# The token factor of the second RMS norm applied to the up projection's sums in PSUM, and another order of the first pairs

## The reference

```python
x = x + jnp.einsum('bse,ed->bsd', y_mix, w_out[l])          # output projection, "OUT"
h = rms_norm(x, norm2_g[l])                                  # x * rsqrt(mean(x*x) + eps) * g
u = causal_dwconv(jnp.einsum('bsd,df->bsf', h, w_up[l]), ffn_conv_w[l])
gate, up = jnp.split(u, 2, axis=-1)
x = x + jnp.einsum('bsf,fd->bsd', jax.nn.gelu(gate) * up, w_down[l])   # down projection, "DOWN"
return rms_norm(x, final_g)
```

## Time and profile before

| | us |
|---|---|
| median of three executions | 1773.47 |
| lowest, highest | 1772.86, 1775.33 |
| the profiled execution | 1773.04 |
| its span, first to last instruction | 1771.3 |
| mean granted TensorE clock in it | 0.982 |
| PE busy | 1705.1 (96%) |
| VectorE busy | 1179.0 (67%) |
| ScalarE busy | 791.0 (45%) |
| GpSimd busy | 538.3 (30%) |

### The profile page before, as it was taken

One profiled execution on the slowest core, in us unless ns is written; L12 is line 12 of the kernel. 1 busy time (PEld: TensorE's weight loads), 2 busy tenths in 40 slices (PEclk: granted clock), 3 DMA queues, 4 the chain that ended last, 5 costly groups with the idle time before them and its releaser, 6 DMA issues.

```text
span 1771.3 us, 20806 instructions
## 1 busy us (share of the span) xinstructions
PE 1705.1 (96%) x7516; PEld 1383.2 (78%) x7516; DVE 1179.0 (67%) x1406; ACT 791.0 (45%) x1022; POOL 538.3 (30%) x297
## 2 busy tenths in 40 slices
PE   6999999999859999999999999998999999999998
PEld 5888878888647888888888888887878877666786
DVE  6577671379888776676676789885636455666554
ACT  5566631245434444444444444553422155666531
POOL 4222122100055455455553000003433242444320
PEclk9999999999879999999999999998999999999999
DMA  7111112063302322322323965651322220110251
GB/s 252 48 47 36 47 48 72 24 220 114 119 11 85 95 73 81 95 71 83 91 75 107 342 217 186 224 160 42 119 72 71 84 71 24 36 48 25 89 220 71
DMA packets 159896, 176.96 MB, mean 100 GB/s; under 512 B 13390, under 2 KB 114516, under 8 KB 159828
## 3 DMA queue, kind: packets, MB, share of 16 engines
q1 hardware_dynamic: 157524, 167.67, 29.4%
q10 hardware_dynamic: 2304, 8.39, 1.3%
HBM read 140.38 MB, written 35.65 MB: 99 GB/s over the span
## 4 chain that ended last, share of the span: by engine, by line
PE 87%; DVE 7%; ACT 3%; issue 1%; POOL 1%; DMA 0%; DVEq 0%; ACTq 0%
PE ps L895 27%; PE ps L2282 25%; PE ps L2230 19%; PE ps L2481 5%; PE ps L2451 3%; PE ps L2466 2%; PE ps L2511 2%; PE ps L2454 2%; PE ps L2453 1%; DVE lat L1993 1%; DVE hop_lo_P L1802 1%; PE ps L2438 1%; DVE hop_mix_P L1796 1%; DVE square_dve L1580 0%; DVE scr L1737 0%
## 5 line engine op out<-in xcount | busy, mean ns | idle before, releaser
L919 POOL TENSOR_TENSOR w_lo<-w_raw,w_hi 128x1024 fp32r<-128x1024 f32 x52 | 136.0, 2617 | 622.5 <-ACT w_hi L1035 622.5
L2282 PE MATMUL ps<-hop_hi_P,wop_hi_P 128*128 128x512 f32 x672 | 266.9, 397 | 25.8 <-DVE hop_lo_P L1802 12.8
L2282 PE MATMUL ps<-hop_lo_P,wop_hi_P 128*128 128x512 f32 x672 | 265.8, 395 | 0.0
L2282 PE MATMUL ps<-hop_hi_P,wop_lo_P 128*128 128x512 f32 x672 | 265.3, 395 | 0.0
L895 PE MATMUL ps<-h_hi,w_hi 128*128 128x512 f32 x752 | 235.6, 395 | 13.3 <-DVE h_lo L1565 9.8
L895 PE MATMUL ps<-h_lo,w_hi 128*128 128x512 f32 x752 | 233.7, 392 | 0.0
L895 PE MATMUL ps<-h_hi,w_lo 128*128 128x512 f32 x752 | 233.4, 392 | 0.0
L925 POOL TENSOR_TENSOR wop_lo_P<-pair_raw,wop_hi_P 128x512 fp32r<-128x512 f32 x72 | 113.3, 1574 | 243.6 <-ACT wop_hi_P L1046 243.5
L895 PEld LDWEIGHTS ps<-h_hi,w_hi 128*128 128x128 f32 x752 | 142.0, 190 | 44.9 <-issue 15.9
L2282 PEld LDWEIGHTS ps<-hop_hi_P,wop_hi_P 128*128 128x128 f32 x672 | 128.7, 192 | 55.1 <-issue 13.6
L925 POOL TENSOR_TENSOR wop_lo_P<-pair_sum,wop_hi_P 128x512 fp32r<-128x512 f32 x96 | 132.0, 1376 | 125.4 <-ACT wop_hi_P L1046 125.4
(11 more groups left out here) (337 smaller groups left out, 3274.4 us busy)
## 6 DMA issues: line engine op xcount, KB each, us to landing
pair_raw<-in_w_up SPq DMA_DIRECT2D x48, 512.0 KB, 4.7
w_raw<-in_w_in SPq DMA_DIRECT2D x46, 512.0 KB, 3.9
dn_raw<-gu_park SPq DMA_DIRECT2D x84, 256.0 KB, 3.9
dn_raw<-in_w_down SPq DMA_DIRECT2D x60, 256.0 KB, 3.1
gu_park<-up_cv SPq DMA_DIRECT2D x24, 512.0 KB, 2.6
out_raw<-in_w_out SPq DMA_DIRECT2D x30, 256.0 KB, 3.0
x_tok<-in_x SPq DMA_DIRECT2D x4, 1024.0 KB, 8.0
x_park<-xs SPq DMA_DIRECT2D x1, 4096.0 KB, 14.7
```

The source lines that it names most:

```text
L919: nc.gpsimd.tensor_tensor(lo[:, :], raw[:, :], hi[:, :].bitcast(f32), ALU.subtract).then_inc(w_lo_done, 1)
L2282: mm = nc.tensor.matmul(dst, w[q][:, k, :], x[q][:, k, :], start=a, stop=b, skip_group_check=True)
```

## The change

- **The norm is taken apart.** ScalarE multiplies x1 by the gain alone (`gained`), partly between the last steps of OUT, into `xs` and, for B22, into `hop_mix["P3"]`. The token factor is spread once for all 1024 tokens, copied by ScalarE from `ps[3]` into SBUF (`rstd_row`, in the T2 half of `xs` tiles 4 and 5), and VectorE multiplies the sums in PSUM with it, 128x1024 in place, once for the gate and once for the up part of each pair (`scale`), ahead of `ff_first`.
- **The squares** of all but the first quadrant are added in three instructions of 128x1024 (`half_squares`) and the rest of the sum is made by PE (`total_squares`: 12 and 16 matmuls with one column). There is one root and one reciprocal.
- **The order of the first pairs** on PE is P1(0), P2(0), P1(1), mean, P5(0), P2(1), mean, P6(0), spread, P5(1), P7(0), P6(1), P4(0), P3(0), P7(1), P4(1), P3(1), P1(2), P6(2), P5(2), P2(2), P7(2), then the loop's order as before. P7's difference is made before P6's, and P6's from it.
- **Splits.** The low parts of the first eleven weight operands (up to P3 of pair 0) and all `hop_lo` are made on VectorE; GpSimd begins with P7 of pair 1. `u2` has two buffers.
- **VectorE's order in a pair**: the weight sums 0 and 1 stand behind C21 and the gate's scaling, in place of behind C22. In pair 0 the whole queue is written out (`first_period`).
- **Transfers.** x1's first four tiles are parked one by one; the reloads of x1 are by halves, the T2 halves of tiles 0 to 6 at the steps 9 to 15 of DOWN, the T1 halves of tiles 0 to 3 at the steps 25 to 28. Slice 4 of DOWN is prepared in the last pair, ahead of its taps.

The diff, cut to its core:

```diff
-        SUMS = ("U2", "U3", "C22", "C21", "C12")
+        SUMS = ("U2", "U3", "C22", "C21", "gate", "C12", "up")
...
-        FIRST_TURNS = tuple((q, n) for n in (0, 1) for q in ("P1", "P2")) + \
-            tuple((q, 0) for q in ("P6", "P5", "P7", "P4", "P3")) + (("P6", 1), ("P5", 1))
+        FIRST_TURNS = (("P1", 0), ("P2", 0), ("P1", 1), ("P5", 0), ("P2", 1), ("P6", 0), ("P5", 1), ("P7", 0), ("P6", 1),
+                       ("P4", 0), ("P3", 0), ("P7", 1), ("P4", 1), ("P3", 1), ("P1", 2))
+        BY_VECTOR = FIRST_TURNS.index(("P7", 1))
...
+        rstd_row = xs[:, 4:6, T2]
...
-            sp.wait_ge(product_added, OUT.added(14))
-            sp.dma_start(x1_park[0:4].rearrange("c p t -> p c t"), x1_early[:, :, :]).then_inc(x1_parked[0], 16)
+            for d in range(4):
+                sp.wait_ge(product_added, OUT.added(11 + d))
+                sp.dma_start(x1_park[d], x1_early[:, d, :]).then_inc(x1_parked[0], 16)
...
+            def gained(c, t):
+                dst = hop_mix["P3"][:, c - 4:c - 3, :] if c >= 4 and t == T2 else xs[:, c:c + 1, t]
+                nc.scalar.activation(dst, x1_tiles(OUT, c, 1, t), ACT.Identity, scale=col(V_NORM2 + c)).then_inc(v_done, 1)
...
-            for n in (0, 1):
-                for q in ("P1", "P2"):
-                    part_low(q, Pair(0, n))
-            for q in ("P6", "P5"):
-                part_low(q, Pair(0, 0))
-            part_low("P7", Pair(0, 0))
-            for h in range(2):
-                hop_low("P3", h)
...
+            pool.wait_ge(wop_lo_done, BY_VECTOR)
...
-            def normed(c, t):
-                V.scalar_tensor_tensor(out=xs[:, c:c + 1, t], in0=x1_tiles(OUT, c, 1, t), scalar=col(V_NORM2 + c),
-                                       in1=ps[3][:, t].unsqueeze(1), op0=ALU.mult, op1=ALU.mult).then_inc(v_done, 1)
...
+            def half_squares(n):
+                dve.wait_ge(x1_square, OUT.square(4 * n + 4))
+                tiles = xs[:, 4:8, T2] if n == 2 else x1_sq2_all
+                V.tensor_tensor(tiles[:, 0:2, :], tiles[:, 0:2, :], tiles[:, 2:4, :], ALU.add).then_inc(x1_squares, 1)
...
+            dve.wait_ge(v_done, 24)
+            hop_add(*t1, (1,))
+            hop_low("P5", (0,))
+            first_low("P1", 1)
+            half_squares(1)
+            hop_low("P5", (1,))
+            first_low("P5", 0)
+            hop_add(*t3)
+            hop_add("P6", lambda h: part_of("B11", h), lambda h: hop_raw("P7", h), ALU.add)
+            half_squares(2)
+            first_low("P2", 1)
+            half_squares(3)
+            dve.wait_ge(x1_parked[0], 64)
+            hop_add("P4", lambda h: part_of("B21", h), lambda h: hop_raw("P6", h), ALU.subtract)
+            hop_low("P6")
+            first_low("P6", 0)
+            dve.wait_ge(root_done, 2)
+            V.reciprocal(rstd[:, :], small[:, 8:16]).then_inc(rstd_done, 1)
+            pair_sums(Pair(0, 1), (0,))
+            hop_low("P7")
+            first_low("P5", 1)
+            dve.wait_ge(x1_parked[1], 16)
+            first_low("P7", 0)
+            second_sum(Pair(0, 0))
+            pair_sums(Pair(0, 1), (1,))
+            hop_low("P3")
+            first_low("P6", 1)
+            hop_low("P4")
+            first_low("P4", 0)
+
+            def scale(pair, name):
+                dve.wait_ge(sums_done, sums({"gate": "C21", "up": "C12"}[name], pair))
+                banks = ps[2 * pair.par + (1 if name == "gate" else 0)][:, :].rearrange("p (j t) -> p j t", j=2)
+                V.tensor_tensor(banks, banks, rstd_row, ALU.mult).then_inc(sums_done, 1)
...
+            def first_period():
+                k = Pair(0, 0)
+                scale(k, "gate")
+                dve.wait_ge(product, nth("P3", k))
+                V.tensor_tensor(bank(k, "c"), bank(k, "c"), u2[0][:, :], ALU.add).then_inc(sums_done, 1)
+                scale(k, "up")
+                third_sums(k.plus(1))
+                taps(k, 0)
+                taps(k, 1)
+                pair_sums(k.plus(2), range(4))
+                gate_up(k)
...
             def period(k):
...
+                scale(k, "gate")
+                if known(k, 2):
+                    pair_sums(k.plus(2), (0, 1))
                 taps(k, 0)
                 dve.wait_ge(product, nth("P3", k))
-                V.tensor_tensor(bank(k, "c"), bank(k, "c"), u2[:, :], ALU.add).then_inc(sums_done, 1)
+                V.tensor_tensor(bank(k, "c"), bank(k, "c"), u2[k.par][:, :], ALU.add).then_inc(sums_done, 1)
...
+                scale(k, "up")
+                if the(k, PAIRS - 1):
+                    slice_low(DOWN, 4)
```

More of the change, by code:

```diff
@@ L966, in _ @@
                     part_low("P7", k.plus(1))
-                if known(k, 2):
+                if known(k, 2) and not the(k, 0):
                     part_low("P1", k.plus(2))
@@ L1333, in _ @@
                     part_high("P3", k.plus(1))
+                if the(k, 0):
+                    part_high("P1", k.plus(2))
+                if the(k, PAIRS - 1):
+                    act.wait_ge(product, nth("P3", LAST))
+                    slice_high(DOWN, 4)
                 ff_first(k, 1)
@@ L1352, in _ @@
                     slice_high(DOWN, 3)
-            act.wait_ge(product, nth("P3", LAST))
-            for n in range(4, DOWN.steps):
+            for n in range(5, DOWN.steps):
                 slice_high(DOWN, n)
@@ L1810, in second_sum @@
                 dve.wait_ge(product, nth("P6", pair))
-                if not the(pair, 0):
-                    dve.wait_ge(sums_done, sums("C12", pair.plus(-1)))
-                from_first(pair, u2)
+                if not isinstance(pair.n, int) or pair.n >= 2:
+                    dve.wait_ge(sums_done, sums("C12", pair.plus(-2)))
+                from_first(pair, u2[pair.par])
             def part_of(name, h):
                 return token_part(name, h)
-            for p in range(2):
-                last_block(OUT, p)
-                add_square(OUT, 12 + p)
@@ L2297, in _ @@
[L2297 to L2305 removed]
+            run("P2", one, True)
+            run("P1", two)
+            pe.wait_ge(x1_squares, squared(OUT, 5))
+            total_squares(0, [square_at(OUT, 0)[2]] + squares_of(1)).then_inc(ms_done, 1)
@@ new lines, in _ @@
+            pe.wait_ge(product_added, OUT.added(14))
+            run("P5", one, True)
+            pe.wait_ge(s1c_done, 2)
+            run("P2", two)
+            pe.wait_ge(x1_squares, squared(OUT, 7))
+            total_squares(4, squares_of(2) + squares_of(3)).then_inc(ms_done, 1)
+            run("P6", one, True)
+            pe.wait_ge(rstd_done, 2)
+            spread(ps[3]).then_inc(rb_done, 1)
+            run("P5", two)
+            pe.wait_ge(sums_done, sums("U2", one))
+            run("P7", one, True)
@@ L2306, in _ @@
+            pe.wait_ge(rstd_spread, 1)
+            run("P6", two)
             for k in periods(pe):
                 after = k.plus(1)
-                if known(k, 1) and not the(k, 0):
+                if known(k, 1) and not the(k, 0) and not the(k, 1):
                     opened(after, "P1")
```

372 lines of the change are left out of this document (197 added, 175 removed).

## The result

The changed kernel takes 1788.2 us (median of 4 runs, 1786.8 to 1790.1) against 1773.9 (1772.9 to 1775.3) before: ratio 1.008, 95% interval 1.0064 to 1.0096. I forecast 1749.5. The profiled execution has a span of 1786.5 us, 15.2 more than before.

What follows compares the result with a forecast made beforehand. PE is busy 96%, but VectorE sets the passage's pace. Gain 26.5 - 1.3 (loop) - 0.5 (down projection) - 0.7 (hand-overs) = 24.0 us from 1773.04: 1749.0, as median 1749.5; range 1743.5 to 1754.5.

Steps and rivals of the forecast that it cites:

- The passage: From output projection to the up projection's first pairs: P7(2) starts at 537.1 instead of 565.8; gain 28.7 - 2.2 = 26.5 us.
- The wait of 3.5 us for U2(2): Before P7(2), VectorE is behind: U2(2) comes at 537.0, PE waits 3.5 us, then loses some 2.2 us to lower clock.
- the wait of 2.5 us for P2's weights: In the passage before P4(0), PE waits 2.5 us for VectorE's weight split for pair 1, then about 2.1 us lower clock.
- the sum: Whole kernel: 26.5 - 1.3 - 0.5, less 0.7 for uncounted hand-overs in the passage, a gain of 24.0 us.
- The ends: Passing into the down projection, later sums and loads cost 0 to 2 us, taken as 0.5.
- The loop: Up-projection pairs: two added scalings raise VectorE's work from 13.31 to 15.7 of 19.05 us; 0.06 us lost per pair, 1.3 us in 21.
- the ring: One pair's walk from P4 through C21, scalings, sums, taps and product to U3 at 21.65, which the next P4 wants at 21.77.
- two waits of 0.6 us for GpSimd: At the end of each pair's VectorE chain, weight sums and product done at 20.9 us, with two waits of 0.6 us.
- The limit: In each pair, the next P4 wants U3 at 19.05 + 2.72 = 21.77 us after P7's end.
- Rival 3: VectorE bounds the loop at U3, SBUF operations behind the scalings meeting GpSimd: gain 8 to 18 us (0.12) or slower (0.04).
- its slower half: Loop loss above 1.15 us a pair turns the change slower; at 1.5 us a pair 1781 us; chance 0.04.
- reserve of 0.1 us: Before U3 in each pair, VectorE's slack falls from about 3 us to 0.1 us.

Runs made afterwards that it cites:

- run 2: Changed kernel with each pair's gate-up product moved on VectorE behind U3 and C22 of the next pair, reference complete: 1751.7 us, ratio 0.9874 to the kernel before.
- run 8: Changed kernel with the product late in the loop, the first pair's behind pair 2's second sum, the last two pairs' at their own ends: 1748.4 us, ratio 0.9859.
- experiment 4: Changed kernel with the up part's scaling cut to 128x768, to 128x512, or left out: 1779.1, 1755.0 and 1749.0 us.

## Why the prediction was wrong, step by step

**The passage: right in its total, with two sizes wrong.** I had P7(2) 28.7 us earlier, less 2.2 us for the clock, that is 26.5; measured are 28.0 and, at the start of P1(3), 26.3. VectorE begins U3(0) at 505.30, where I had 505.4. The wait of 3.5 us for U2(2) was 2.75, and the lower clock behind it cost 1.7 us. PE doesn't wait for the root, as said. But P4(0) starts at 507.75, not at 506.5, and PE's way there is not the one I counted. The two groups of sums of squares take 2.6 and 3.5 us (480.10 to 482.69, 489.87 to 493.36), not 1.3 and 1.7: the eight small rows of 1.05 us in the earlier trace rows are four matmuls of the program, so its 12 and 16 stand in the trace as 24 and 32. Behind each group matmuls come 0.43 us apart, and P5(0) and P6(0) take 4.4 us instead of 2.72. Against that, the wait of 2.5 us for P2's weights with its 2.1 us of lower clock didn't come. That these errors left only 1.25 us is luck. With the loop repaired, the gain is 22.2 us (run 2) and 25.7 us (run 8) where the sum had 24.0.

**The ends: right.** I gave 0 to 2 us of waits at the start of the down projection; it was 0.9.

**The loop: wrong, and with it the sign.** I walked the ring from C21 at 5.5 to U3 at 21.65: a chain of 16.15 us. The measured one is 17.71. Up to the end of the second taps the walk is good to 0.15 us at each step (at its end 12.1 us from C21 against 12.05), scalings included (1.23 us for 1.22). Two terms failed.
- *"Weight sums and product behind two waits of 0.6 us for GpSimd".* I priced a meeting by the one lengthened sum of the earlier trace rows, 1.26 instead of 0.69, as a fixed toll. It is the rest of whatever operation GpSimd has running, and where GpSimd has further splits queued, each VectorE operation lets one in before the next. The three operations waited 0.43, 1.09 and 1.10 us, together 2.6, not 1.2. That is 1.4 of the 1.56 us by which the chain is longer.
- *The limit.* I held 16.15 against 21.77 - 5.5 = 16.27. Behind a wait, P4 to C21 takes 3.06 us and the hand-over 0.13, so the limit is 15.86. My own chain would have been late by 0.29 us a pair, 6 us in all, rather than by 0.06.

Together 1.56 + 0.29 = 1.85 us a pair; measured 1.84 in the middle of the loop, where I had 0.06.

**Rival 3 was the truth, and I gave its slower half 0.04.** I named the mechanism, its place and the point from which it decides (1.15 us a pair), and had 1.5 us a pair giving 1781. What spoke for it was a reserve of 0.1 us, one thirtieth of the one before, laid over 21 repetitions, with four to five exposed operations behind it. What I set against it, VectorE's idle time in a period, is no argument in a ring: the idle time is the wait for P4 and can't be spent on the way to it. The reserve of 0.1 us was smaller than the 0.4 us by which my hand-overs were off (16.27 against 15.86), and that deserved far more than 4 in 100.

**What the trace before could have told.** In its period the product starts at 737.97, GpSimd's split right behind it:

```profile
738.26 2.08 POOL L925 TENSOR_TENSOR wop_lo_P<-pair_raw,wop_hi_P 128x512 fp32r<-128x512 f32 x1 [1.36 <-ACT wop_hi_P L1046]
```

The split took 2.08 us instead of 1.29, the product its plain 1.21. VectorE won that meeting by 0.29 us. The change pushes it from 11.3 us behind C21 (737.97 - 726.67) to 14.8, into a row of splits, and nothing said that it would win there too. The Trainium skill (SBUF — State Buffer, section "Who interferes with whom") has the sentence that I left unused: "Issue order, not op shape, decides who blocks". The traces of experiment 4 agree: 0.13 us behind the split the product takes 2.31 us, 0.12 us ahead of it 1.21.

## What to carry to other kernels

Walk the ring of a repeated stage (who waits for whom until it closes) and hold its length against the pace-setting engine; busy shares and idle time say nothing about it. Where an added operation eats the reserve of such a ring, look at every operation of the shared SBUF path behind it: pushed by a fraction of a microsecond, it may lose a race that it used to win, and then waits for the other engine's whole operation, in every period. The cure cost nothing here: an operation that isn't on the ring belongs behind the last one that is, where the engine idles anyway.

## What the runs showed of the hardware

- Two-input SBUF operations of VectorE and GpSimd's splits shut each other out in whole operations and in strict turn: with three splits in a row, three VectorE operations grew by 0.43, 1.09 and 1.10 us, and the splits from 1.29 to 1.74 and 1.64. The scalings, with one input in PSUM, stayed at 1.23 us throughout.
- The effect has a threshold: 0.27 us less work per pair changed the period by 1.38 us (20.62 to 19.24).
- Of PE's waits in the changed kernel from P7(2) on, the clock fell behind the first alone: after 2.75 us without a matmul eight matmuls came 0.43 us apart, the 1.2 GHz level (granted 0.56 from 538 to 541 us); after 1.70 and 1.55 us it stayed at 1.00. It fell without a wait too, during or behind 2.6 and 3.5 us of one-column matmuls (0.83 from 480 to 490 and from 490 to 500 us).
- A wait of TensorE costs a little more than its length: after 1.55 us of waiting the period was 1.84 us longer. From the last matmul's start to the first after the wait are 1.94 us, 1.71 more than the usual 0.227, and the matmuls behind it come 0.33, 0.24 and 0.23 us apart, at a granted clock of 1.00 over the period.
